# The weight-side remainders of a down projection, moved from VectorE to GpSimd

## The reference

```python
def conv_gated_mlp(h, w_up, conv_w, conv_b, w_down):
    ...
    a, v = jnp.split(uc, 2, axis=-1)
    return jnp.einsum('btf,fd->btd', jax.nn.gelu(a) * v, w_down)
# in third_block:
        h = layer_norm_3(ALPHA * h + ffn, ln2_g[l], ln2_b[l])
```

## Time and profile before

| | us |
|---|---|
| median of 3 runs (lowest to highest) | 2840.54 (2839.1 to 2843.41) |
| the profiled execution | 2836.5 |
| its span | 2834.7 |
| TensorE busy in the span | 2709.8 (96%) |
| VectorE busy | 2120.4 (75%) |
| ScalarE busy | 1039.6 (37%) |
| GpSimd busy | 490.9 (17%) |
| down projection, first matmul (L3428) to the end of the span | 2613.1 to 2834.7 |

### The profile page before, as it was taken

How to read it: one execution, slowest core, us unless ns; L and a number is a source line. 1 busy time by engine, 2 the same in 40 slices (tenths; PEclk the granted TensorE clock), 3 DMA queues, 4 the chain that set the end, 5 groups by cost and what they waited for, 6 DMA issues and landing times. The chain is left out here.

```text
span 2834.7 us, 33511 instructions
## 1 busy us (share of the span) xinstructions
PE 2709.8 (96%) x13192; PEld 2206.6 (78%) x13192; DVE 2120.4 (75%) x2797; ACT 1039.6 (37%) x1503; POOL 490.9 (17%) x260
## 2 busy tenths in 40 slices
PE   6999999999999989899999889999989999999998
PEld 5888888878888768588776578878878788888887
DVE  6989997864625671599987875698176988887978
ACT  5111112143414331412127641377231555555333
POOL 0000000000100011002220100345120466665000
PEclk9999999999999999999999999999999999999999
DMA  5212221224335551011110032100122222224531
GB/s 235 97 61 88 92 82 60 100 103 127 97 112 171 162 171 52 30 60 45 45 61 12 31 119 88 51 25 25 56 91 103 79 85 75 89 82 161 196 97 60
DMA packets 97998, 253.32 MB, mean 89 GB/s; under 512 B 7265, under 2 KB 34273, under 8 KB 96178
## 3 DMA queue, kind: packets, MB, share of 16 engines
q1 hardware_dynamic: 93298, 234.63, 24.2%
q10 hardware_dynamic: 4288, 15.73, 1.4%
q0 software_dynamic: 256, 0.82, 0.1%
HBM read 206.07 MB, written 45.09 MB: 89 GB/s over the span
## 5 line engine op out<-in xcount | busy, mean ns | idle before, releaser
L369 PE MATMUL pair<-u_hi,w_hi 128*128 128x512 f32 x768 | 301.9, 393 | 1.2 <-PEq L92 0.9
L634 DVE SCALAR_TENSOR_TENSOR conv_acc<-aT,cols,conv_acc 128x1024 f32<-128x1024 f32 x232 | 297.9, 1284 | 6.7
L370 PE MATMUL pair<-u_lo,w_hi 128*128 128x512 f32 x768 | 299.8, 390 | 0.0
L371 PE MATMUL pair<-u_hi,w_lo 128*128 128x512 f32 x768 | 299.8, 390 | 0.0
L369 PEld LDWEIGHTS pair<-u_hi,w_hi 128*128 128x128 f32 x768 | 145.0, 189 | 32.6 <-issue 2.4
L1829 DVE TENSOR_SCALAR_CACHE_REDUCE counted<-choice,top_i 128x384 uint8<-128x384 f32 (+2 forms) x192 | 169.2, 942 | 0.0
L370 PEld LDWEIGHTS pair<-u_lo,w_hi 128*128 128x128 f32 x768 | 144.9, 189 | 30.8 <-issue 0.7
L371 PEld LDWEIGHTS pair<-u_hi,w_lo 128*128 128x128 f32 x768 | 144.8, 189 | 30.3
L369 PE MATMUL pair<-h_hi,ch_hi 128*128 128x512 f32 x400 | 159.7, 399 | 4.6 <-DVE h_lo L1448 2.4
L370 PE MATMUL pair<-h_lo,ch_hi 128*128 128x512 f32 x400 | 157.3, 393 | 0.0
L371 PE MATMUL pair<-h_hi,ch_lo 128*128 128x512 f32 x400 | 157.2, 393 | 0.0
(11 more groups left out here) (482 smaller groups left out, 7043.8 us busy)
## 6 DMA issues: line engine op xcount, KB each, us to landing
wt<-in_w_ch SPq DMA_DIRECT2D x60, 512.0 KB, 3.4
wo_raw<-in_w_out SPq DMA_DIRECT2D x48, 512.0 KB, 3.5
wt<-in_w_up SPq DMA_DIRECT2D x10, 1024.0 KB, 4.9
w_raw<-in_w_up SPq DMA_DIRECT2D x10, 1024.0 KB, 4.9
g_spill<-g_stage SPq DMA_DIRECT2D x40, 256.0 KB, 2.2
ada_mod<-in_ada_mod SPq DMA_DIRECT2D x4, 2048.0 KB, 14.5
wt<-in_w_conv SPq DMA_DIRECT2D x16, 512.0 KB, 3.4
qk<-qk_st SPq DMA_DIRECT2D x8, 1024.0 KB, 6.5
```

Source lines behind the costliest of these rows:

```text
L369: nc.tensor.matmul(bank, w[0], x[0], start=(first and k == 0), stop=False)
L370: nc.tensor.matmul(bank, w[0], x[1], start=False, stop=False)
L371: return nc.tensor.matmul(bank, w[1], x[0], start=False, stop=(last and k == n_k - 1))
L634: nc.vector.scalar_tensor_tensor(dst, x, w, conv_acc[:], ALU.mult, ALU.add).then_inc(conv_step, 1)
```

## The change

The subtraction that makes `w_lo` is taken out of VectorE's `low` for all chunks and put into a new `low` of `down_gpsimd`, in a queue order of its own; VectorE's `low` keeps `x_lo`. The semaphore `dn_lo_ok` becomes two, `dn_w_lo` (raised by GpSimd) and `dn_x_lo` (raised by VectorE), each of which counts one per chunk. Whoever waited for both remainders of a chunk now waits for both semaphores (`lows_done`); TensorE waits for `dn_w_lo` ahead of the second kind and for `dn_x_lo` ahead of the third. GpSimd's list has the chunks of P2 in the order 2, then (after P3) 0, 1, 3, 4, 5, as VectorE's.

```diff
--- before.py
+++ after.py
@@ -2839,8 +2839,8 @@
         sd_d, rv_d = small7[:, 56:60], small7[:, 60:64]
         ld_a = [sem(f"ld_a{c}") for c in range(NC)]
         ld_b = [sem(f"ld_b{c}") for c in range(NC)]
-        dn_hi_ok, dn_lo_ok, dn_lo_first, dn_sum, dn_used, dn_mm, dn_res, dn_vec = (sem(x) for x in (
-            "dn_hi_ok", "dn_lo_ok", "dn_lo_first", "dn_sum", "dn_used", "dn_mm", "dn_res", "dn_vec"))
+        dn_hi_ok, dn_x_lo, dn_w_lo, dn_lo_first, dn_sum, dn_used, dn_mm, dn_res, dn_vec = (sem(x) for x in (
+            "dn_hi_ok", "dn_x_lo", "dn_w_lo", "dn_lo_first", "dn_sum", "dn_used", "dn_mm", "dn_res", "dn_vec"))
         xd_in = [sem(f"xd_in{g}") for g in range(2)]
         dn_var, dn_sd, dn_own, dn_h, dn_out = (sem(x) for x in ("dn_var", "dn_sd", "dn_own", "dn_h", "dn_out"))
 
@@ -2854,7 +2854,11 @@
             return 2 * HI_ORDER.index((p, c))
 
         def lo_count(p, c):
-            return 2 * LO_ORDER.index((p, c))
+            return LO_ORDER.index((p, c)) + 1
+
+        def lows_done(eng, p, c):
+            eng.wait_ge(dn_w_lo, lo_count(p, c))
+            eng.wait_ge(dn_x_lo, lo_count(p, c))
 
         def w_sum_count(p, c):
             return SUM_COUNT[("w", p, c)]
@@ -3334,10 +3338,10 @@
                 sp.dma_start(xc[c], gated_tiles(1, FH + 2 * c, n_of(c))).then_inc(ld_b[c], 16)
             residual(1)
             for c in range(NC):
-                sp.wait_ge(dn_lo_ok, lo_count(P5, c) + 2)
+                lows_done(sp, P5, c)
                 sp.dma_start(wa[c], weight_tiles(0, FH + 2 * c, n_of(c))).then_inc(ld_a[c], 16)
                 sp.dma_start(xa[c], gated_tiles(0, FH + 2 * c, n_of(c))).then_inc(ld_a[c], 16)
-            sp.wait_ge(dn_lo_ok, lo_count(P4, 1) + 2)
+            lows_done(sp, P4, 1)
             sp.dma_start(lg_d[:], bcast(a["ln2_g"], 0, D)).then_inc(dn_vec, 16)
             sp.dma_start(lb_d[:], bcast(a["ln2_b"], 0, D)).then_inc(dn_vec, 16)
             for t in range(NG):
@@ -3352,7 +3356,7 @@
             x_hi, _, w_hi, _ = dn_slot(p, c)
             if p == P2 and c >= 2:
                 freed = {2: (P4, 3), 3: (P3, 3), 4: (P3, 3), 5: (P3, 4)}[c]
-                act.wait_ge(dn_lo_ok, lo_count(*freed) + 2)
+                lows_done(act, *freed)
             elif n >= 2:
                 act.wait_ge(dn_used, n - 1)
             else:
@@ -3402,6 +3406,22 @@
                 pool.wait_ge(dn_hi_ok, hi_count(P1, c) + 2)
                 nc.gpsimd.tensor_tensor(x_lo, xa[c], x_hi.bitcast(F32), ALU.subtract).then_inc(dn_lo_first, 1)
 
+            def low(p, c):
+                _, _, w_hi, w_lo = dn_slot(p, c)
+                pool.wait_ge(dn_hi_ok, hi_count(p, c) + 1)
+                nc.gpsimd.tensor_tensor(w_lo, w_side[p][c], w_hi.bitcast(F32), ALU.subtract).then_inc(dn_w_lo, 1)
+
+            for c in range(2, NC):
+                low(P1, c)
+            for p in (P7, P6, P5, P4):
+                for c in range(NC):
+                    low(p, c)
+            low(P2, 2)
+            for c in range(NC):
+                low(P3, c)
+            for c in (0, 1, 3, 4, 5):
+                low(P2, c)
+
         def down_tensor(pe):
             def bank_free(p, t):
                 if p == P1:
@@ -3419,7 +3439,9 @@
                 if (p, c) in DONE_FIRST:
                     pe.wait_ge(dn_lo_first, 2 * c + i)
                 else:
-                    pe.wait_ge(dn_lo_ok, lo_count(p, c) + i)
+                    pe.wait_ge(dn_w_lo, lo_count(p, c))
+                    if i == 2:
+                        pe.wait_ge(dn_x_lo, lo_count(p, c))
 
             def tile_products(p, c, kind, t):
                 x_hi, x_lo, w_hi, w_lo = dn_slot(p, c)
@@ -3476,11 +3498,9 @@
                 return tile(t)[:, h * HALF:(h + 1) * HALF]
 
             def low(p, c):
-                x_hi, x_lo, w_hi, w_lo = dn_slot(p, c)
-                dve.wait_ge(dn_hi_ok, hi_count(p, c) + 1)
-                nc.vector.tensor_tensor(w_lo, w_side[p][c], w_hi.bitcast(F32), ALU.subtract).then_inc(dn_lo_ok, 1)
+                x_hi, x_lo, _, _ = dn_slot(p, c)
                 dve.wait_ge(dn_hi_ok, hi_count(p, c) + 2)
-                nc.vector.tensor_tensor(x_lo, x_side[p][c], x_hi.bitcast(F32), ALU.subtract).then_inc(dn_lo_ok, 1)
+                nc.vector.tensor_tensor(x_lo, x_side[p][c], x_hi.bitcast(F32), ALU.subtract).then_inc(dn_x_lo, 1)
 
             def sums_7(c):
                 dve.wait_ge(ld_a[c], 32)
@@ -3490,7 +3510,7 @@
 
             def sums_6(c):
                 dve.wait_ge(ld_b[c], 64)
-                dve.wait_ge(dn_lo_ok, lo_count(P7, c) + 2)
+                lows_done(dve, P7, c)
                 nc.vector.tensor_tensor(xb[c], xc[c], xb[c], ALU.subtract).then_inc(dn_sum, 1)
                 nc.vector.tensor_tensor(wb[c], wb[c], wa[c], ALU.add).then_inc(dn_sum, 1)
 
@@ -3501,7 +3521,7 @@
 
             def sum_4(c):
                 dve.wait_ge(ld_a[c], 64)
-                dve.wait_ge(dn_lo_ok, lo_count(P6, c) + 2)
+                lows_done(dve, P6, c)
                 dve.wait_ge(dn_sum, w_sum_count(P5, c))
                 nc.vector.tensor_tensor(wb[c], wa[c], wb[c], ALU.subtract).then_inc(dn_sum, 1)
```

## The result

| | before | changed |
|---|---|---|
| median of 4 runs, us | 2840.39 | 2855.46 (2851.2 to 2856.67) |
| the profiled execution, us | 2836.5 | 2856.3 |
| its span | 2834.7 | 2854.5 |
| down projection, first matmul to the end of the span | 221.6 | 234.9 |
| GpSimd busy | 490.9 | 592.6 |

The ratio is 1.0048, 95% interval 1.0036 to 1.0060: slower, by 15.1 us of the medians against 13.1 predicted (2855.5 against 2853.6). Of the 19.8 us between the two spans 6.5 lie ahead of the down projection, which the change doesn't touch (it begins at 2619.63 instead of 2613.08, and at 2614.4 in the second profile). So from here on I compare the stage: 221.6 before, 234.9 after, 13.3 more.

The account below looks back on a forecast made before the run. It took the stage to be bound by TensorE, VectorE bounding only its last 23 us. Stalls 2.3 + 2.0 + 2.8 + 2.8 + 3.2 = 13.1 us gave 2853.6 against the median 2840.54; range 2845 to 2861.

Parts of the forecast that it names:

- 1, P7 chunk 0: P7 chunk 0: VectorE's `x_lo` late by 4.8 us, so TensorE stalls 2.3.
- 2, P7 chunk 5: P7's sixth chunk: `x_lo` late by 5.7 us, ended 2675.1, so TensorE stalls 2.0.
- 3, P5 chunk 0: Start of P5: P6's sums that free P5's banks come late, so TensorE stalls 2.8 us.
- 4, P3 chunk 0: P3 chunk 0: `x_lo` 4.8 us later, ended 2766.96, wanted 2769.04, so TensorE stalls 2.8.
- 5, P2 chunk 1: P2 chunk 1: `x_lo` 6.5 us later, TensorE stalls 3.0, plus 0.2 of handing over: 3.2.
- The price: VectorE work with two SBUF operands is held up 2.2 us by a wide GpSimd `w_lo`, 1.1 by a narrow one.
- both cases: Start of P5: `w_lo` of P5 chunk 0 ahead of the sums, stall 3.3; just behind, 2.2 less; 2.8 taken.
- The clock: Rival: stalls lower TensorE's clock; two drops on top of the sum give 2857; two or more, chance 0.07.
- Nothing lost: Rival: VectorE's idle time takes up the whole exclusion; price 0, 2840.5 us; nothing or nearly nothing lost, chance 0.12.
- the longer: Rival: turns cost more than 2.2, say 2.5; P7's chunks fall behind; 19 us, 2859.5; chance 0.08.
- the shorter blocking: Rival: turns cost 2.1; 10 us, 2850.5; chance 0.70 together with the forecast and one clock drop at most.
- a lock of the whole recorded 2.4: The skill's rule, VectorE blocked for GpSimd's whole 2.4 us: about 15 us at the five places instead of 13.1.

Follow-up runs that it names:

- the second execution: The changed kernel, nothing altered, run and profiled once more: 2853.02 us, ratio 1.0050 against the kernel before, stage 234.5.
- The semaphores alone: The changed kernel with every `w_lo` made by VectorE again, split semaphores and double waits kept: 2840.75 us, ratio 0.9996, stage 221.7.
- the idle subtractions: The kernel before plus 30 GpSimd subtractions in P7 to P3 on a buffer nobody reads: 2857.17 us, ratio 1.0062, stage 240.2.
- the memsets: The kernel before plus 30 GpSimd memsets of a buffer nobody reads, in P7 to P3: 2839.98 us, ratio 1.0001, stage 221.7.
- another order: The changed kernel with GpSimd's P2 and P3 remainders reordered, VectorE's queue likewise, two norm steps behind P2 chunk 1: 2852.64 us, ratio 1.0046, stage 232.0.
- the halves: The changed kernel with each wide `w_lo` cut into two GpSimd subtractions of 128x512: 2850.94 us, ratio 1.0039, stage 230.5.

## Why the prediction was right, and where it was not

The mechanism held: GpSimd's reading holds VectorE up by 2.2 us a turn, and TensorE waits for a late `x_lo` at a few places. The total held too, 13.1 against 13.3 in the stage, but in part by luck: of the 13.3 only 8.9 are the waits that it was added up from.

| place | predicted | changed kernel | again |
|---|---|---|---|
| 1, P7 chunk 0 | 2.3 | 2.61, then half clock 1.7 | 2.61, then 0.84 for `w_lo` |
| 2, P7 chunk 5 | 2.0 | none | none |
| 3, P5 chunk 0 | 2.8 | 0.97 | 1.0 |
| 4, P3 chunk 0 | 2.8 | 2.74 | 2.74 |
| 5, P2 chunk 1 | 3.2 | 2.84, then half clock 1.9 | 2.86, then half clock |

*The price.* 2.2 for a wide remainder and 1.1 for a narrow one were right to a hundredth: 3.41 against 1.21 again and again, sums from PSUM at 0.68. The semaphores alone, the idle subtractions and the memsets show that GpSimd's reading is what makes VectorE late.

*Places 1 and 4* were right within 0.3, the time and the place. So was place 5's wait, but not what follows it.

*Place 2 did not come.* `x_lo` of the sixth chunk ended 25.90 us into P7 before; I had it 5.7 later. It was 4.2 later in the changed kernel (2680.13, TensorE at 2681.79) and 3.7 in the second execution, and TensorE was by then late by 4.5 and 4.1 itself, from the wait at chunk 0 and what followed it. I take it that `w_hi` so came later and GpSimd asked less often at a bad moment: I had kept GpSimd's requests at the times of before. The experiment with another order leaves P7 alone, and nothing followed the 2.61 at chunk 0 there: the same `x_lo` ended at 2682.81, 31.88 into the pass and 6.0 late, and TensorE, late by only 2.9, waited 1.70, which is place 2 nearly as predicted. I take it that tenths in who asks first decide, which no run singles out. In the changed kernel P7's loss of 4.5 equals the 4.3 predicted for places 1 and 2, but from half clock in place of the second: the agreement is luck in part.

*Place 3 was mis-sized*, 2.8 for 1.0. I had given both cases, the first with `w_lo` of P5 chunk 0 ahead of the sums, and chose that because it is asked for 1 us ahead of them. VectorE and GpSimd of the changed kernel:

```profile
2713.01 1.21 DVE L3520 TENSOR_TENSOR wa<-wc,wb 128x1024 f32<-128x1024 f32 x1
2714.14 2.47 DVE L3539 SCALAR_TENSOR_TENSOR xd<-xd,pair 128x512 f32<-128x512 f32 x4
2716.54 3.40 DVE L3503 TENSOR_TENSOR dn_x_lo<-xa,dn_x_hi 128x1024 fp32r<-128x1024 f32 x1
```

```profile
2713.65 5.21 POOL L3412 TENSOR_TENSOR dn_w_lo<-wa,dn_w_hi 128x1024 fp32r<-128x1024 f32 x2 [4.52 <-ACT dn_w_hi L3370]
```

GpSimd asks at 2713.65, while VectorE has the port for an operand sum; it gets it at 2714.14, when VectorE goes over to the four sums from PSUM. These run at full speed beside it (2.47 for four, 2.66 in the earlier trace rows). So the sums paid nothing and TensorE waited 0.3 for them, as before; the `x_lo` behind them paid, and TensorE waited 0.70 for it. Being asked for ahead of a PSUM sum costs that sum nothing, and by the earlier trace rows I knew it: the error was to charge the turn to the sums at all. Without that turn my figure would have been 1.1, near the measured 1.0 by its number only: it had TensorE wait for the sums, and it waited for the `x_lo` behind them.

*The clock* was a rival with 0.07 for two drops, on top of the sum. Two came, with 3.6 us, not on top of the sum but in the gap of 3.8 that places 2 and 3 left: so the total, too, is right in part by luck. The length of the wait alone does not decide. Behind 2.61 at P7 chunk 0 it fell once and stayed three times (the second execution, the kernel with P1 and P7 moved, the one with another order). Behind 2.74 at P3 chunk 0 it stayed both times. Behind 2.84 to 2.86 at P2 chunk 1 it fell all three times, behind 2.17 at P3's sixth chunk (another order) and behind 1.99 at P7's (the halves) it fell too, and behind 1.70 there it stayed. In the kernel with the idle subtractions it fell behind waits of 2.39, 4.04 and 3.00. What does decide, these runs leave open.

*The rivals.* "Nothing lost" is refuted for the whole and right for P5 and P4. Of the longer and the shorter blocking neither came: the price was 2.20. For a lock of the whole recorded 2.4 the prediction gave about 15 in all; its own terms with 2.4 (and 1.2 for a narrow one) give 3.2 + 2.7 + 4.1 + 3.5 + 4.0 = 17.5, and with 2.1 about 11 where it said 10. The forecast itself, with 2.2, is not touched by that.

## What to carry to other kernels

Before work is given to an idle engine, look for a row where the two engines run side by side and compare it with the same shape alone: here 3.95 against 1.76, in another stage of the same kernel, gave 2.19 us an operation, and 2.20 came. Then charge that price only to the operations that use the shared port, in the order of the queue, and only where the engine has no slack: moved in P5 and P4 alone the work was free, and elsewhere the loss fell on one or two waits of a pass. And price a new stall of TensorE with what may follow it: up to 1.9 us of half clock, less what that hides.

## What the runs showed of the hardware

- A GpSimd subtraction shuts out a VectorE operation with two SBUF operands for nearly all of its time: 2.20 us for 128x1024, 1.10 for 128x512, 1.7 when both of its operands are one buffer (and it takes 1.89 then, not 2.4). The norm's wide steps are held up like the subtractions (two in 6.74 us instead of 2.48). The engines take turns operation by operation; a memset of GpSimd (0.96 us) shuts out nothing.
- VectorE operations that read PSUM and one SBUF operand pass beside GpSimd at full speed: four in 2.47 us.
- One wait of 2 to 4 us in a TensorE stream that is otherwise full is at times followed by about eight matmuls at 1.2 GHz (8 in 3.65 us instead of 2.08), and at times not, at the same place of the same kernel.
